# Reordering a few vector, scalar and GpSimd steps beside the matmuls of a hybrid attention block

## The reference

```python
h = rmsnorm(x, norm_mix)
qa, ka, va, ga, cq, ckv, kr, gb = split(h @ w_in)
# group A: 8 heads of 64, 2 kv groups, |t - s| <= 128, in blocks of 128 queries by up to 384 keys
scores = q @ k.T / 8 - slope * |t - s|
m = max(max(scores), sink);  p = exp(scores - m);  p /= sum(p) + exp(sink - m)
ya = (p @ v) * silu(ga)
# group B: 8 heads, dense, q and k of 64 plain and 32 rotary columns made from low-rank cq, ckv
yb = (softmax((qn @ kn.T + qr @ kr.T) * 96 ** -0.5) @ vb) * silu(gb)
x = x + concat(ya, yb) @ w_out
out = rmsnorm(x, final_norm)
```

## Time and profile before

| | us |
|---|---|
| median of 3 runs (625.22 to 625.94) | 625.66 |
| the profiled execution's own time | 625.79 |
| its span | 624.0 |
| TensorE matmul (PE) busy | 614.7 |
| VectorE (DVE) busy | 440.5 |
| ScalarE (ACT) busy | 355.0 |
| GpSimd (POOL) busy | 319.7 |
| TensorE clock granted, share of full | 0.999 |

### The profile page before, as it was taken

One profiled execution on the slowest core, in us unless ns is written; L12 is line 12 of the kernel. 1 busy time (PEld: TensorE's weight loads), 2 busy tenths in 40 slices (PEclk: granted clock), 3 DMA queues, 4 the chain that ended last, 5 costly groups with the idle time before them and its releaser, 6 DMA issues.

```text
span 624.0 us, 9407 instructions
## 1 busy us (share of the span) xinstructions
PE 614.7 (99%) x3255; PEld 502.2 (80%) x3255; DVE 440.5 (71%) x852; ACT 355.0 (57%) x763; POOL 319.7 (51%) x309
## 2 busy tenths in 40 slices
PE   8999999999999999999999999999999999999996
PEld 7889888888888887888887777777777777888885
DVE  4673326333444439998998789989898898799684
ACT  6662223223334227767776678787787878532563
POOL 4634004403656532546546776887788789610701
PEclk9999999999999999999999999999999999999999
DMA  7640016366676720101015733323423423499033
GB/s 247 197 143 1 0 52 233 128 254 186 221 265 220 235 67 1 34 2 35 1 27 132 214 69 82 71 60 81 98 61 76 102 85 136 137 348 358 0 147 124
DMA packets 49934, 76.90 MB, mean 123 GB/s; under 512 B 5656, under 2 KB 25632, under 8 KB 49760
## 3 DMA queue, kind: packets, MB, share of 16 engines
q1 hardware_dynamic: 49728, 76.04, 39.1%
q10 hardware_dynamic: 160, 0.27, 0.1%
HBM read 46.54 MB, written 20.05 MB: 107 GB/s over the span
## 4 chain that ended last, share of the span: by engine, by line
PE 93%; DVE 4%; ACT 2%; issue 1%; POOL 0%; POOLq 0%; ACTq 0%
PE ps L1535 18%; PE ps L1537 17%; PE ps L1536 17%; PE ps L1825 9%; PE ps L1757 4%; PE ps L1762 4%; PE ps L1843 4%; PE ps L1842 4%; PE ps L1727 3%; PE ps L1777 2%; PE ps L1737 2%; PE ps L1738 1%; PE ps L1716 1%; PE ps L1715 1%; PE ps L1547 1%; PE ps L1587 1%
## 5 line engine op out<-in xcount | busy, mean ns | idle before, releaser
L1389 DVE TENSOR_TENSOR pT_lo<-ps,pT_hi 128x512 fp32r<-128x512 f32 x128 | 87.9, 690 | 16.9 <-ACT pT_hi L1015 16.6
L1015 ACT ACTIVATE pT_hi<-ps 128x512 fp32r<-128x512 f32 x128 | 75.9, 596 | 37.6 <-PE ps L1825 37.3
L742 POOL TENSOR_SCALAR p_b<-p_b,stat 128x1024 f32<-128x1024 f32 x64 | 71.8, 1122 | 37.8 <-DVE stat L1384 37.8
L1535 PE MATMUL ps<-hT_hi,w_hi 128*128 128x512 f32 x208 | 84.0, 404 | 0.0
L1537 PE MATMUL ps<-hT_hi,w_lo 128*128 128x512 f32 x208 | 81.4, 391 | 0.0
L1536 PE MATMUL ps<-hT_lo,w_hi 128*128 128x512 f32 x208 | 81.0, 390 | 0.0
L1825 PE MATMUL ps<-ident,p_b 128*128 128x128 f32 x512 | 78.2, 276 | 0.5 <-DVE pT_lo L1389 0.4
L1825 PEld LDWEIGHTS ps<-ident,p_b 128*128 128x128 f32 x512 | 60.6, 140 | 22.2 <-issue 8.1
L1379 DVE TENSOR_REDUCE stat<-ps 128x1 f32<-128x1024 f32 x64 | 77.7, 1215 | 0.8 <-PE ps L1777 0.6
L1004 ACT ACTIVATE p_b<-ps,stat 128x1024 f32<-128x1024 f32 x64 | 71.3, 1114 | 6.9 <-DVE stat L1379 3.2
L1842 PE MATMUL ps<-pT_hi,vB 128*128 128x512 f32 x128 | 55.4, 433 | 0.0
(11 more groups left out here) (216 smaller groups left out, 1477.7 us busy)
## 6 DMA issues: line engine op xcount, KB each, us to landing
w_raw<-w_in SPq DMA_DIRECT2D x13, 512.0 KB, 4.6
x_in<-x SPq DMA_DIRECT2D x8, 512.0 KB, 3.5
wt_raw<-w_out SPq DMA_DIRECT2D x8, 512.0 KB, 4.5
t_scratch<-wt_hi SPq DMA_DIRECT2D x16, 256.0 KB, 2.4
t_scratch<-wt_lo SPq DMA_DIRECT2D x16, 256.0 KB, 2.6
q<-q_h SPq DMA_DIRECT2D x16, 256.0 KB, 3.6
wn_raw<-w_in SPq DMA_DIRECT2D x8, 336.0 KB, 3.7
k<-k SPq DMA_DIRECT2D x9, 256.0 KB, 3.0
```

Of the source, the lines that this page charges most:

```text
L742: nc.gpsimd.tensor_scalar(p_b[:, (U + 1) % 4, :], p_b[:, (U + 1) % 4, :], r_b[:, U % 4:U % 4 + 1], 0.5, ALU.mult, ALU.mult).then_inc(s_bp, 1)
L1015: nc.scalar.activation(pT_hi[:, 1 - G % 2, 4 * a:4 * a + 4, U % 4 * P:(U % 4 + 1) * P], ps[:, 4 + a, :].rearrange("p (k c) -> p k c", c=P) ...
L1389: nc.vector.tensor_tensor(pT_lo[at_], ps[:, 4 + a, :].rearrange("p (k c) -> p k c", c=P), f(pT_hi[at_]), ALU.subtract).then_inc(s_bTl, 1)
L1535: nc.tensor.matmul(o, a_hi, b_hi, start=first, stop=False, skip_group_check=goes_on)
```

## The change

Nothing is computed otherwise; steps change their place in the lists of their engines.

1. GpSimd, step 15: the lo part of the first dense k was made in two halves, one before `probs_w(15)` and one after `gate_w(13)`. It is now one instruction over all 1024 columns, behind `probs_w(15)` and before `gate_w(13)`.
2. ScalarE and VectorE, step 3: the hi part of the first key block goes ahead of the first `exp_w`, its lo part ahead of the second `max_w`.
3. VectorE, step 1: the lo part of the second key block goes ahead of the fourth `max_w` and `sink_w`.
4. VectorE, U = 8: the last gated evacuation goes ahead of `recip_b(9)` and `pT_b_lo(7, 1)`; it was behind both.
5. ScalarE, U = 56 to 62: the four `a_hi` of the first output product stood as 2, 1, 1, 0 in the four pairs; they stand now as 1, 1, 1, 1.

```diff
@@ GpSimd @@
                 nc.gpsimd.tensor_scalar(q_h[:, :], q_raw[:, :], 1.0, 1.0, ALU.mult, ALU.mult).then_inc(s_h0, 1)
+
+            def head0_k_lo():
+
                 pool.wait_ge(s_h0kh, 1)
-
-            def head0_k_lo(c):
-                return nc.gpsimd.tensor_tensor(k_2[0:HD, 0, c], k_raw[0:HD, c], f(k_1[0:HD, 0, c]), ALU.subtract)
+                nc.gpsimd.tensor_tensor(k_2[0:HD, 0, :], k_raw[0:HD, :], f(k_1[0:HD, 0, :]),
+                                        ALU.subtract).then_inc(s_h0k, 1)
...
                 if s == W_UNITS - 1:
                     head0_hi()
-                    head0_k_lo(slice(0, HALF))
                 if s < W_UNITS:
                     probs_w(s)
+                if s == W_UNITS - 1:
+                    head0_k_lo()
                 if s >= 2:
                     gate_w(s - 2)
                 if s in (3, 7, 11):
                     split_w(NM - 3 + (s - 3) // 4)
-                if s == W_UNITS - 1:
-                    head0_k_lo(slice(HALF, SEQ)).then_inc(s_h0k, 1)
@@ ScalarE @@
                 if s >= 2:
                     o_w_lo(s - 2)
+                if s == 3:
+                    pT_w_hi(keys[0])
                 if live:
                     exp_w(s, 0)
                 else:
                     first_v_hi()
                 for i, c in enumerate(keys[:2]):
-                    pT_w_hi(c)
+                    if s != 3 or i:
+                        pT_w_hi(c)
                     if live:
                         exp_w(s, 1 + i)
...
                 if U == B_UNITS - 8:
                     act.wait_ge(s_wy, W_UNITS)
                     act.wait_ge(s_bs, B_UNITS - NT)
-                    a_hi(P1, 0, A11)
-                    a_hi(P1, 1, A11)
-                if U in (B_UNITS - 6, B_UNITS - 4):
-                    a_hi(P1, (U - (B_UNITS - 6)) // 2 + 2, A11)
+                if U >= B_UNITS - 8:
+                    a_hi(P1, (U - (B_UNITS - 8)) // 2, A11)
@@ VectorE @@
                 if s >= 2:
                     o_w_sum(s - 2)
+                if s == 3:
+                    pT_w_lo(keys[0])
                 if live:
                     max_w(s, 1)
                 if not live:
                     head0_lo()
-                if s >= 1:
+                if s >= 1 and s != 3:
                     pT_w_lo(keys[0])
                 if live:
                     max_w(s, 2)
+                if s == 1:
+                    pT_w_lo(keys[1])
+                if live:
                     max_w(s, 3)
                     sink_w(s)
-                if s >= 1:
+                if s >= 2:
                     pT_w_lo(keys[1])
...
+                if U == 8:
+                    evac_g(2 * NM - 1)
                 recip_b(U + 1)
                 if U >= 2:
                     pT_b_lo(U - 1, 1)
-                if U == 8:
-                    evac_g(2 * NM - 1)
```

## The result

| us | before | after |
|---|---|---|
| median of 22 runs each | 625.65 (625.04 to 626.94) | 626.63 (625.97 to 627.74) |
| span of the profiled execution | 624.0 | 625.3 |

The ratio after to before is 1.0017 [1.0011, 1.0023]: the change costs about 1.0 us. The forecast was 627.0, with an own range from 626.6 to 627.5.

A forecast was written before the change was run, and what follows sets the result against it. The prediction took TensorE to bound the kernel (busy 614.7 of 624.0 us), the banded stage being a closed loop. Terms 0.55 + 0.60 + 0.87 - 0.40 - 0.28 = +1.34 on 625.66 gave 627.0 us, range 626.6 to 627.5.

The forecast's parts named there:

- Step 1: Banded stage: lo part ahead of the fourth maximum delays ScalarE, sum and reciprocal; TensorE waits at step 2's transposes; +0.55 us.
- Step 3: Banded stage: inserted lo part delays the second maximum and ScalarE's packed list; first product's stall goes, later products late; +0.60 us.
- Nothing gives it back: Steps 4 to 14: every engine starts from the late scores of step 4, so step 3's +0.60 us stays.
- Rival 2: Steps 1 and 3: the loop has unseen slack and the stalls simply go; 624.8 us; chance 0.08 alone.
- Step 15: Steps 15 and 16: freed sink subtraction gains 0.67, but head0_lo waits for the whole GpSimd k; net +0.87 us.
- rival 1: Step 16: VectorE's q subtraction gets the port before GpSimd's k, so the 0.67 gain stays; 625.5 us; chance 0.13.
- border of 0.2%: What a measurement can tell from no change, 1.25 us; slower begins at 626.9 us.
- U = 8: Dense stage: the last gated evacuation moves to where VectorE idles, so the 6.46 us pair becomes plain at 6.07; -0.40 us.
- U = 56: Dense stage: hi parts as 1, 1, 1, 1 make the 6.34 us pair plain at 6.06 or 6.07; -0.28 us.
- Rival 3: Dense stage: heavy transfers make the two slow pairs, so the 0.68 isn't gained; 627.7 us; chance 0.11.

The follow-up runs named there:

- spare instruction: Kernel before plus an unused VectorE reduction in step 6 ahead of the second maximum and in step 9 behind the probabilities: 626.2 us, +0.40 from step 7 on.
- parts 2 and 3 alone: Two kernels: the kernel before with only the step 3 edit, 626.01 us, ratio 1.001; and with only the step 1 edit, 625.87 us, ratio 1.0005.
- part 1 alone: Kernel before with only the GpSimd edit, the first dense k's lo part as one instruction behind the probabilities of step 15: 626.26 us beside 625.55, ratio 1.0013.
- halves: Kernel before with the k subtraction behind the probabilities of step 15 as two instructions of 512 columns in a row: 626.44 us beside 625.53, ratio 1.0016.
- quarters: Kernel before with the k subtraction behind the probabilities of step 15 as four instructions of 256 columns in a row: 625.75 us beside 625.0, net +0.53.
- 4+5: Kernel before with only the two dense edits, the evacuation at U = 8 and the hi parts 1, 1, 1, 1: 624.85 us, ratio 0.999.
- behind gate: Kernel before with the undivided k subtraction behind gate_w(13): 625.17 us, ratio 0.9996.
- behind gate and dense: Kernel before with the undivided k subtraction behind gate_w(13) and the two dense edits, without the edits of steps 1 and 3: 624.25 us, ratio 0.9983.
- with increment: Kernel before with two k subtractions in a row behind the probabilities, the first incrementing a semaphore nobody waits for: 626.28 us beside 625.36, ratio 1.0014.
- with increment and dense: Kernel before with two k subtractions in a row, the first incrementing a semaphore, and the two dense edits: 625.47 us beside 625.36, ratio 1.0001.
- half, gate, half: Kernel before with one k subtraction of 512 columns without an increment, then gate_w(13), then the other: 625.75 us, net +0.39.

## Why the prediction was right

Its mechanisms held point by point, and the time came out 0.4 below its centre; the sum was +1.34, and the traces give +0.96. All five terms were off in the same direction, the three costs too large and the two gains too small, so the measured 626.63 lies only just inside its own range, whose lower end was 626.6.

- **Step 1, +0.55 predicted, +0.43 to +0.45 measured.** The chain was the right one, down to the wait for GpSimd's probabilities at the transposes of step 2. The term is too big by 0.1: the lo part started with the read of the maximum's result (both at 236.77), not 0.05 behind it; the sum for the reciprocal came 238.62 - 237.76 - 0.34 = 0.52 later; and the maximum of step 2 then followed VectorE's probabilities after 0.76, where it was 0.83 before, so it came only 0.45 later. The spare instruction points the same way: 0.47 of VectorE inside the way cost 0.41.
- **Step 3, +0.60 predicted, +0.51 measured.** The first exponential was met at +0.60 as said; the ones behind it slipped by 0.50. Before, the exponential stood waiting for its maximum; now it follows the hi part without a wait and starts 0.10 before that one's recorded end (see the last section). "ScalarE's list is packed behind it" was right, but the packing is tighter than starts that followed a wait had shown.
- **Nothing gives it back.** Shown: the difference stays at +1.27 from 252 to 330 us, the idle time before the first maximum stays 0.63, and the spare instruction's +0.40 is still +0.39 at 330 us. Rival 2 (loose stalls that simply go) is refuted by parts 2 and 3 alone, each of which removed its stall and had TensorE later behind it, not earlier (+0.51 and +0.43).
- **Step 15, +0.87 predicted, +0.81 (after) and +0.79 (alone) measured.** The gain was put at 0.67 and is 0.66. q was to start 0.28 behind k and did so by 0.30, so rival 1 (VectorE first) did not come up, in after or in part 1 alone (0.28 there). k took 2.39 where 2.45 was taken from a wider form; q ended 1.08 after k, as the row of before had it; q was to be over 3 us long and is 3.17.
- **U = 8, -0.40 predicted, -0.43; U = 56, -0.28 predicted, -0.32.** Rival 3 is refuted by equal pairs at 0.68 and 0.78 of the DMA engines.
- **Where the choice was hard.** With +1.34 the forecast lay 0.1 above the border of 0.2% (1.25 us), and the measured +1.0 lies 0.2 below it. The prediction gave "slower" 0.48 and "same" 0.45, so its favourite by a narrow margin was not what was measured. The terms of steps 1 and 3, together 0.2 too large, decided the side. A sum whose terms are each good to 0.1 can't tell the sides of a border that lies 0.1 away.

On the port, the prediction had weighed a rule of the Trainium skill (page "SBUF — State Buffer", section "SBUF: two separate sides"), that whoever starts first has the shared port for the whole instruction. The undivided k and the gate agree: q is 3.17 us long beside the one and 1.54 beside the other, and in the other direction the undivided k takes 3.37 instead of 2.39 when q is ahead of it. The halves and quarters go beyond it: q stood through two, and through three, whole instructions.

## What to carry to other kernels

In a step that is a closed loop (its first instruction waits for the engine that waits for its last), both lo parts that were moved ahead here only exchanged a stall for a later and longer one. Ask whether the way round the loop gets shorter, and put what TensorE doesn't wait for behind the last instruction that it does wait for, where the spare instruction cost nothing. A VectorE subtraction with two SBUF operands that started beside a GpSimd instruction on SBUF operands lasted here at least for the rest of that instruction and then 1.08 us (q), so look at which one starts beside which: with k behind the short gate the kernel was 0.3 faster than before, with k in front of it, undivided or in halves, 0.8 to 1.0 slower. The two stalls in the dense stage, where no such loop closes, were worth their full time, and one instruction moved elsewhere in the same list was enough to get it.

## What the hardware showed beyond that

**VectorE is not let in at every border.** The times are from the start of q to the end of the GpSimd instruction that was running. The kernels of parts 2, 3, 4+5 and the spare instruction meet as before does, at 0.30 or 0.31:

| kernel | GpSimd instruction that ended | us after q's start | q let in |
|---|---|---|---|
| before; behind gate; behind gate and dense | gate, 128x256 | 0.30; 0.46; 0.45 | yes |
| quarters | first k piece, 64x256 | 0.45 | no |
| halves; with increment; with increment and dense | first k piece, 64x512 | 1.01; 1.01; 0.99 | no |
| half, gate, half | k piece, 64x512 | 0.99 | no |
| quarters | second k piece, 64x256 | 1.13 | no |
| half, gate, half | gate behind it, 128x256 | 1.68 | yes |
| quarters | third k piece | 1.83 | yes |
| after; undivided k alone | k, 64x1024 | 2.09 | yes |
| halves; with increment; with increment and dense | second k piece, 64x512 | 2.26; 2.25; 2.24 | yes |

Once let in, q ran 1.08 us every time, and the GpSimd instruction behind that border waited for it. The increment doesn't decide, nor does what kind of instruction comes next, nor the end of any instruction as such. The time q has waited doesn't decide alone either: a gate let it in after 0.30, a quarter didn't after 0.45 nor after 1.13. What decides **stays open**. In these runs q never got in behind a k piece of 64x512 or less before it had waited 1.8 us.

That isn't true of VectorE in general. The sink subtraction of before got in behind the first 64x512 half after 0.81, where GpSimd had nothing to do next, and the lo part of v behind the undivided k after 0.97, where a gate came next. Late in the kernel before, VectorE also got in between two GpSimd subtractions of one kind in a row, after 1.16: a multiplication of 128x512 with two SBUF inputs, which takes 0.68 undisturbed, ends 0.55 after the first, and the second takes 1.74 where some 1.3 is usual. The kernel before, GpSimd and then VectorE:

```profile
591.19 1.29 POOL L771 TENSOR_TENSOR sa_bl<-wo_raw,sa_bh 128x512 fp32r<-128x512 f32 x1
592.44 1.74 POOL L771 TENSOR_TENSOR sa_bl<-wo_raw,sa_bh 128x512 fp32r<-128x512 f32 x1
...
591.32 1.71 DVE L1497 TENSOR_TENSOR acc_b<-acc_b,g_fin 128x512 f32<-128x512 f32 x1
```

So a row of equal GpSimd instructions doesn't by itself keep VectorE out. These pieces had 128 partitions and those of k 64; whether that matters was not tried.

**Activations overlap when nothing is awaited.** In after the hi part at 249.77 was 0.58 long and the exponential behind it started at 250.24, 0.10 before the recorded end at 250.35. ScalarE:

```profile
249.77 0.58 ACT L949 ACTIVATE pT_wh<-ps 128x512 fp32r<-128x512 f32 x1
250.24 0.60 ACT L938 ACTIVATE p_w<-p_w,stat 128x384 f32<-128x384 f32 x1
```

The kernel before shows the same in many places: in its step 3, for example, the sink's exponential starts at 250.18, 0.09 before the recorded end of the instruction ahead of it (250.08 + 0.19). So this part of the error of step 3 could have been read ahead: a chain taken from starts that each followed a wait came out too long by some 0.1 where the change took such a wait away.
